# Row normalisation of attention probabilities moved from GpSimd to VectorE, in a two-layer decoder trunk on one Trainium2 core

## The chip, the core and the metric

The kernel runs on one core of one Trainium2 chip. A core has TensorE (PE, matrix products; its weight loads are listed as PEld), VectorE (DVE), ScalarE (ACT), GpSimd (POOL) and SyncE (SP, which only issues transfers here). They run side by side, each with its own queue of instructions in a fixed order, and wait for one another through semaphores. The metric is the time of the whole kernel on the device in microseconds (us).

## The reference

Two residual layers on x of 1024 positions x 1024 channels, fp32: a gated short convolution, and then forgetting attention with 16 heads of 64. The change is in the second. Per head and block of 128 queries:

```python
s = jnp.einsum('bhqd,bhkd->bhqk', qb, k) * scale
s = s + cb[..., :, None] - c[..., None, :]
s = jnp.where(kpos[None, :] <= qpos[:, None], s, neg)
p = jax.nn.softmax(s, axis=-1)
return jnp.einsum('bhqk,bhkd->bhqd', p, v)
```

`c` is a running sum of log forget gates. Before it lie an RMS norm and one projection to q, k, v, an output gate z and the forget gates, q and k being RMS-normalised per head; behind it the gating by silu(z) and an output projection that is added to x.

## The kernel before, in words

Every fp32 product is made from three TensorE products: an operand is split into a "hi" part (rounded, made by ScalarE) and a "lo" part (the rest, a subtraction on VectorE or GpSimd). So each tile of weights, h, probabilities, q, k and v has a hi and a lo.

The attention layer is software-pipelined over head pairs. Iteration `it` (0 to 8) projects q, k, z and v of pair `it` (`proj`, iterations 0 to 7) and does the attention of pair `it` - 1 (`att`, iterations 1 to 8); iterations 2 to 6 or 7 are a hardware loop on each engine. A pass has 8 steps `i`: four for each of the two heads of the pair ("side"), with query super-blocks t = 3, 2, 1, 0 of 256 rows, each as two blocks `par` 0 and 1 of 128 queries, whose rows have 128 (2t + 1 + par) keys: 896 and 1024 columns in steps 0 and 4, 640 and 768 in 1 and 5, 384 and 512 in 2 and 6, 128 and 256 in 3 and 7.

What happens to a block (step i, block par): TensorE makes the scores in PSUM (L722). VectorE adds the mask (L1657) and takes the negated row maximum (L1663). ScalarE takes the exponential into `p_big` (even steps) or `p_small` (odd steps) and sums each row into `denom` (L1170). VectorE inverts it (`invert`, L1671, semaphore `s_rd`), and GpSimd multiplies the row by the inverse (`normalise`, L1934, semaphore `s_pn`). In the next step TensorE transposes the normalised blocks in chunks of 256 keys (L739, waits for `s_pn` of both blocks), ScalarE makes `pt_hi` (L1180), VectorE makes `pt_lo` (`pt_low`, L1677), and TensorE multiplies by v, "pv" (L758, waits for `s_ptl`). ScalarE and VectorE collect the output (L1190, L1684), and VectorE gates it (L1693).

In each step TensorE's queue has, in this order: scores of block 0, two or three pieces of projection (L575), transposes of the previous step's first two chunks, more projection, in steps 2 to 5 the head mean squares (L774, L775), scores of block 1, and then pv, transposes and projection in turn. VectorE's queue has mask and maximum of block 0, an evacuation of a projection (L1735, L1749), `invert` of block 0, the first `pt_low`, mask and maximum of block 1, the other `pt_low`, the gating, `invert` of block 1, and in steps 2 to 5 a Newton refinement (`refine`, L1714 to L1722) of the head norms, in whose middle the mask and maximum of the next step's block 0 are put:

```python
if att:
    invert(it, i, 0)
for c in range(min(2, chunks)):
    pt_low(own, at, c)
```

GpSimd's queue has per pass the 16 `normalise`, four `w_low` (lo part of a weight tile, L1925), four `square_lo` (L1939) and two `stack_k_lo` (L1945). At the end of iteration 7 VectorE makes h_lo of four gated output tiles (`y2_low`, L1807), and GpSimd two in iteration 8 (L1952). All loads are issued by SyncE.

Of the kernel before, what the change touches and what calls it, by code (L numbers as in the profile page):

```python
# [7 lines left out]
ALU = mybir.AluOpType  # L8
# [3 lines left out]
P = 128  # L12
# [13 lines left out]
N_FORGET, N_AIN, N_AOUT = 0, 1, 4 * KT + 1  # L26
# [33 lines left out]
STEPS = [(x, t) for x in range(2) for t in (3, 2, 1, 0)]  # L60
# [4 lines left out]
def keys(t, par):  # L65

    return P * (2 * t + 1 + par)
# [48 lines left out]
def hybrid(nc, x, w_cin, w_cout, w_ain, w_forget, w_aout, conv_gain, conv_taps, attn_gain, b_forget,  # L116
# [5 lines left out]
    with ExitStack() as ctx:  # L122
# [23 lines left out]
        rdenom = sb("rdenom", [P, 4])  # L146
# [44 lines left out]
        p_big = sb("p_big", [P, 2, S])  # L191
# [31 lines left out]
        p_small = sb("p_small", [P, 2, 3 * P * 2])  # L223
# [54 lines left out]
        s_wlo = sem("w_lo_made")  # L278
# [30 lines left out]
        s_rd = sem("denominators_inverted")  # L309
        s_pn = sem("p_normalised")  # L310
# [1028 lines left out]
        def _(dve):  # L1339
# [325 lines left out]
            def invert(it, i, par):  # L1665
                pair = it - 1
                col = 2 * (i % 2) + par
                dve.wait_ge(s_exp, 16 * pair + 2 * i + par + 1)
                if counted(16 * pair + 2 * i + par - 3):
                    dve.wait_ge(s_pn, 16 * pair + 2 * i + par - 3)  # L1670
                v.reciprocal(rdenom[:, col:col + 1], denom[:, col:col + 1]).then_inc(s_rd, 1)  # L1671

            def pt_low(it, at, c):
                pair = it - 1
                g, w = CHUNK0[at] + c, chunk_columns(STEPS[at][1], c)
                dve.wait_ge(s_pth, CHUNKS * pair + g + 1)
                TT(pt_lo[:, g % 2, 0:w], ps[:, B_PT + g % 2, 0:w], pt_hi[:, g % 2, 0:w].bitcast(F32),  # L1677
                   ALU.subtract).then_inc(s_ptl, 1)
# [72 lines left out]
            def iteration(it, proj, att, before, base, last=False):  # L1751
                local = 0
                for i in range(8):
                    own, at = (it, i - 1) if i else (it - 1, 7)
                    chunks = STEPS[at][1] + 1 if (att and i) or (before and not i) else 0
                    if att and not (proj and 3 <= i <= 6):
                        row_max(it, i, 0)
                    if att and i == 0:
                        vz_evac(it - 1, 7)
                    if proj and 1 <= i <= 4:  # L1760
                        qk_evac(it, i - 1)
                    if proj and 5 <= i:
                        vz_evac(it, i - 1)
                    if not proj and i == 2:
                        add_ahead(1)
                    if not proj and i > 2:
                        add_ahead(i - 1)
                    if att:
                        invert(it, i, 0)
                    for c in range(min(2, chunks)):  # L1770
                        pt_low(own, at, c)
                    if att and i == 0:
                        v_low(it - 1, 0)
                    if att:
                        row_max(it, i, 1)
                    if not proj and i == 1:
                        y2_low(6)
                    if att and i == 0:
                        stack_q_lo(it - 1, 1)
                    if att and i == 1:  # L1780
                        v_low(it - 1, 1)
                    for c in range(2, chunks):
                        pt_low(own, at, c)
                    if att and i and STEPS[i - 1][1] in (1, 3) and (i >= 2 or (before and proj)):
                        out_gate(*((it, i - 2) if i >= 2 else (it - 1, 7)))
                    if att:
                        invert(it, i, 1)
                    if proj and 2 <= i <= 5:
                        local = refine(it, i - 2, base, local, i + 1 if att else None)
                    if not att and i in (1, 3, 4, 5):  # L1790
                        forget((1, 3, 4, 5).index(i))
                    if proj and i == (6 if last else 7):
                        stack_q_lo(it, 0)
                    if last and i == 7:
                        for k in range(4):
                            y2_low(k)
                    if chunks and STEPS[at][1] % 2 == 0:
                        out_sum(own, at)
                    if not proj and i == 0:
                        out_gate(it - 1, 7)  # L1800
                    if not proj and i == 1:
                        add_ahead(0)
                return local
# [50 lines left out]
        def _(pool):  # L1854
            g = nc.gpsimd
            TT = g.tensor_tensor
# [68 lines left out]
                TT(w_lo[slot][:, :, :], w_raw[:, slot, :, :], w_hi[slot][:, :, :].bitcast(F32),  # L1925
                   ALU.subtract).then_inc(s_wlo, 1)

            def normalise(it, i, par):
                pair = it - 1
                w = keys(STEPS[i][1], par)  # L1930
                col = 2 * (i % 2) + par
                pool.wait_ge(s_rd, 16 * pair + 2 * i + par + 1)
                p = (p_big if i % 2 == 0 else p_small)[:, par, 0:w]
                TT(p, p, rdenom[:, col:col + 1].broadcast_to([P, w]), ALU.mult).then_inc(s_pn, 1)  # L1934

            def square_lo(it, u):

                pool.wait_ge(s_qsq, 4 * it + u + 1)
# [15 lines left out]
            def iteration(it, proj, att):  # L1954
                for i in range(8):
                    if proj and i % 2 == 0:
                        w_low(N_AIN + 4 * it + i // 2 + 1, (N_AIN + i // 2 + 1) % 2)
                    if not proj and i in (3, 5, 7):
                        n = N_AOUT + 2 + (3, 5, 7).index(i)
                        w_low(n, n % 2)  # L1960
                    if not proj and i == 0:
                        y2_low(4)
                    if att:
                        normalise(it, i, 0)
                    if not proj and i == 0:
                        y2_low(5)
                    if att and i == 1 and proj:
                        pool.wait_ge(s_pn, 16 * it - 13)
                        stack_k_lo(it - 1, 1)
                    if not proj and i == 2:  # L1970
                        pool.wait_ge(s_pn, 16 * it - 11)
                        stack_k_lo(it - 1, 1)
                    if proj and i == 7:
                        if att:
                            pool.wait_ge(s_pn, 16 * it - 1)
                        else:
                            pool.wait_ge(s_wlo, N_AIN + 4 * it + 5)
                        stack_k_lo(it, 0)
                    if att:
                        normalise(it, i, 1)  # L1980
                    if proj and 1 <= i <= 4:
                        square_lo(it, i - 1)
                    if not proj and i == 0:
                        w_low(N_AOUT + 1, (N_AOUT + 1) % 2)
# [50 lines left out]
```

## Time and profile before

| | |
|---|---|
| median of 3 runs | 1135.32 us (1134.02 to 1135.85) |
| profiled execution | 1135.81 us, of which the span is 1134.0 us |
| granted TensorE clock, mean | 0.992 |
| busy: PE, PEld, DVE, ACT, POOL | 1106.5, 916.7, 770.9, 601.4, 565.3 us |

The span is the time from the first to the last instruction. "Busy" counts the time in which an engine works on an instruction. Idle time of an engine costs only where another engine, in the end TensorE, waits for what it makes. The convolution layer fills the first 434 us; iteration 1 begins near 482 us, and the seven passes with both a projection and attention (iterations 1 to 7) last until about 1004.

### The profile page before, as it was taken

To read this page: it belongs to the slowest core of one execution; us is meant where nothing else is said; L and a number is where in the kernel's file an instruction comes from. 1 tells how busy PE (TensorE), PEld (TensorE's weight loads), DVE (VectorE), ACT (ScalarE), POOL (GpSimd) and SP (SyncE) were. 2 spreads that over 40 slices of the span, in tenths; PEclk is the share of its full clock that TensorE was granted. 3 is DMA by queue.
4 is the path that set the end of the run, shared out by engine and by line. 5 is a ranking of instruction groups with operands and counts; after the bars stand their busy time and mean duration, and the time that the engine had idled before them with its cause. 6 is when DMAs were issued, how large, how long until landed. Compare 5 with 4: busy or idle time off the path is not lost.

```text
span 1134.0 us, 16593 instructions
## 1 busy us (share of the span) xinstructions
PE 1106.5 (98%) x5512; PEld 916.7 (81%) x5512; DVE 770.9 (68%) x1180; ACT 601.4 (53%) x1014; POOL 565.3 (50%) x376
## 2 busy tenths in 40 slices
PE   4999999999999999999999999999999999989998
PEld 3787888888888887788888888888888888878887
DVE  5896787567766325667777777686776777876641
ACT  5553233233243324675766767767667676666510
POOL 2235665555563646454555554645546555554420
PEclk8999999999999999999999999999999999989999
DMA  6202101210135402110100110101001101002142
GB/s 223 75 1 75 43 33 75 75 62 14 75 107 174 130 39 93 45 41 20 38 21 19 38 38 19 37 19 38 19 18 38 38 19 37 19 23 90 56 167 75
DMA packets 20257, 64.17 MB, mean 57 GB/s; under 512 B 2928, under 2 KB 3056, under 8 KB 20208
## 3 DMA queue, kind: packets, MB, share of 16 engines
q1 hardware_dynamic: 20064, 63.53, 16.6%
q8 instruction: 28, 0.46, 0.2%
q14 instruction: 21, 0.17, 0.0%
q10 hardware_dynamic: 144, 0.00, 0.0%
HBM read 54.88 MB, written 8.65 MB: 56 GB/s over the span
## 4 chain that ended last, share of the span: by engine, by line
PE 80%; DVE 7%; issue 2%; POOL 2%; ACT 1%; DMA 1%; SPq 0%; ACTq 0%; DVEq 0%; POOLq 0%
PE ps L575 34%; PE ps L589 18%; PE ps L670 6%; PE ps L722 6%; PE ps L758 6%; PE ps L739 6%; POOL p_big L1934 1%; DVE neg_max L1663 1%; PE ps L781 1%; DVE b_lo L1381 1%; DVE h_lo L1807 1%; PE ps L774 1%; PE ps L775 1%; PE ps L694 1%; DMA raw<-in_w_cout 1%
## 5 line engine op out<-in xcount | busy, mean ns | idle before, releaser
L575 PE MATMUL ps<-h_hi,w_hi 128*128 128x512 f32 x632 | 262.9, 416 | 4.0 <-DVE v_t L1749 2.1
L575 PE MATMUL ps<-h_hi,w_lo 128*128 128x512 f32 x632 | 248.6, 393 | 0.0
L575 PE MATMUL ps<-h_lo,w_hi 128*128 128x512 f32 x632 | 248.3, 393 | 0.0
L1870 POOL TENSOR_TENSOR a_lo<-raw,a_hi 128x512 fp32r<-128x512 f32 x94 | 136.7, 1466 | 155.4 <-ACT a_hi L954 155.4
L589 PE MATMUL ps<-b_hi,a_hi 128*128 128x512 f32 x456 | 179.8, 394 | 9.1 <-DVE b_lo L1381 8.5
L589 PE MATMUL ps<-b_lo,a_hi 128*128 128x512 f32 x456 | 178.5, 391 | 0.0
L589 PE MATMUL ps<-b_hi,a_lo 128*128 128x512 f32 x456 | 178.4, 391 | 0.0
L1934 POOL TENSOR_TENSOR p_big<-p_big,rdenom 128x896 f32<-128x896 f32 (+1 forms) x64 | 94.1, 1470 | 96.3 <-DVE rdenom L1671 96.2
L575 PEld LDWEIGHTS ps<-h_hi,w_lo 128*128 128x128 f32 x632 | 118.9, 188 | 27.2
L1934 POOL TENSOR_TENSOR p_small<-p_small,rdenom 128x640 f32<-128x640 f32 (+1 forms) x64 | 72.1, 1127 | 135.4 <-DVE rdenom L1671 135.1
L575 PEld LDWEIGHTS ps<-h_hi,w_hi 128*128 128x128 f32 x632 | 119.6, 189 | 20.9 <-DVE v_t L1749 3.0
L575 PEld LDWEIGHTS ps<-h_lo,w_hi 128*128 128x128 f32 x632 | 119.8, 190 | 14.7 <-issue 0.2
L1925 POOL TENSOR_TENSOR w_lo<-w_raw,w_hi 128x1024 fp32r<-128x1024 f32 x39 | 95.0, 2435 | 62.8 <-ACT w_hi L926 62.8
L954 ACT ACTIVATE a_hi<-raw 128x512 fp32r<-128x512 f32 x94 | 58.1, 628 | 118.5 <-DMA raw<-in_w_cin 44.5
L1677 DVE TENSOR_TENSOR pt_lo<-ps,pt_hi 128x512 fp32r<-128x512 f32 (+1 forms) x160 | 96.7, 629 | 34.6 <-ACT pt_hi L1180 34.0
L589 PEld LDWEIGHTS ps<-b_hi,a_hi 128*128 128x128 f32 x456 | 86.2, 189 | 31.0 <-DVE b_lo L1381 10.9
L589 PEld LDWEIGHTS ps<-b_hi,a_lo 128*128 128x128 f32 x456 | 86.2, 189 | 18.1
L589 PEld LDWEIGHTS ps<-b_lo,a_hi 128*128 128x128 f32 x456 | 86.2, 189 | 17.8 <-issue 0.2
L1663 DVE TENSOR_REDUCE neg_max<-ps 128x1 f32<-128x896 f32 (+7 forms) x128 | 97.0, 758 | 4.4
L1180 ACT ACTIVATE pt_hi<-ps 128x512 fp32r<-128x512 f32 (+1 forms) x160 | 83.1, 551 | 23.8 <-PE ps L739 21.9
L722 PE MATMUL ps<-k,q 128*128 128x512 f32 (+5 forms) x384 | 92.1, 348 | 0.6 <-ACT p_big L1170 0.6
L1657 DVE TENSOR_TENSOR ps<-ps,mask_bf 128x128 f32<-128x128 f32 x128 | 38.0, 297 | 67.1 <-PE ps L722 66.7
(179 smaller groups left out, 2063.7 us busy)
## 6 DMA issues: line engine op xcount, KB each, us to landing
w_raw<-in_w_ain SPq DMA_DIRECT2D x32, 512.0 KB, 3.3
raw<-in_w_cin SPq DMA_DIRECT2D x28, 512.0 KB, 4.3
xy<-in_x SPq DMA_DIRECT2D x16, 512.0 KB, 4.5
raw<-in_w_cout SPq DMA_DIRECT2D x8, 512.0 KB, 4.2
x_dram<-xy SPq DMA_DIRECT2D x8, 512.0 KB, 4.0
w_raw<-in_w_aout SPq DMA_DIRECT2D x8, 512.0 KB, 3.3
out<-y SPq DMA_DIRECT2D x7, 512.0 KB, 7.1
raw<-in_w_cin SPq DMA_DIRECT2D x8, 256.0 KB, 8.6
```

The costliest lines, as they stand in the source:

```text
L575: last = mm(ps[:, bank, :], st[slot][:, k, :], mov(k)[:, halves(h)], start=(at == 0 and (when or k == 0) and st is w_hi and mov is mov_hi) ...
L589: ins = mm(ps[:, bank, :], st[:, i % RING, k, :], mov[:, k, :], start=(first and st is a_hi and mov is b_hi[b]), stop=(last and st is a_lo ...
L670: ins = mm(ps[:, BANKS[u % 8], :], st[:, i, k % KH, :], mov[Y_SLOT + s][:, 2 * c + h, :], start=(first and k == ks[0] and st is a_hi and m ...
L722: last = mm(ps[:, bank, 0:w], a[:, side, qs:qs + P], b[:, side, c * w:(c + 1) * w], start=(a is q1), stop=(a is q2))
L739: last = nc.tensor.transpose(ps[:, B_PT + g % 2, at:at + P], src[:, par, (2 * c + kp) * P:(2 * c + kp + 1) * P], ident[:, :])
L758: last = mm(ps[:, B_OUT, at + skip:at + 2 * P], v_st[:, side, 2 * c + kp, :], mov[:, g % 2, kp * 2 * P:(kp + 1) * 2 * P - skip], start=(c ...
L1180: A(pt_hi[:, g % 2, 0:w], ps[:, B_PT + g % 2, 0:w], ACT.Copy).then_inc(s_pth, 1)
L1663: v.tensor_reduce(neg_max[:, col:col + 1], src, ax, ALU.max, negate=True).then_inc(s_max, 1)
L1677: TT(pt_lo[:, g % 2, 0:w], ps[:, B_PT + g % 2, 0:w], pt_hi[:, g % 2, 0:w].bitcast(F32), ALU.subtract).then_inc(s_ptl, 1)
L1870: TT(a_lo[:, i % RING, :, :], entry_source(i), a_hi[:, i % RING, :, :].bitcast(F32), ALU.subtract).then_inc(s_alo, 1)
L1925: TT(w_lo[slot][:, :, :], w_raw[:, slot, :, :], w_hi[slot][:, :, :].bitcast(F32), ALU.subtract).then_inc(s_wlo, 1)
L1934: TT(p, p, rdenom[:, col:col + 1].broadcast_to([P, w]), ALU.mult).then_inc(s_pn, 1)
```

## The change

`normalise` leaves GpSimd's queue and becomes a `tensor_scalar` of VectorE, issued directly behind each `invert`. It waits for VectorE's own reciprocal (`s_rd`) and counts `s_pn` as before. On GpSimd, three waits for `s_pn` ahead of `stack_k_lo` become waits for earlier `w_low` of the same queue.

```diff
 (VectorE)
+            def normalise(it, i, par):
+                pair = it - 1
+                w = keys(STEPS[i][1], par)
+                col = 2 * (i % 2) + par
+                dve.wait_ge(s_rd, 16 * pair + 2 * i + par + 1)
+                p = (p_big if i % 2 == 0 else p_small)[:, par, 0:w]
+                TS(p, p, rdenom[:, col:col + 1], None, ALU.mult).then_inc(s_pn, 1)
...
                     if att:
                         invert(it, i, 0)
+                        normalise(it, i, 0)
...
                     if att:
                         invert(it, i, 1)
+                        normalise(it, i, 1)
 (GpSimd)
-            def normalise(it, i, par):
-                pair = it - 1
-                w = keys(STEPS[i][1], par)
-                col = 2 * (i % 2) + par
-                pool.wait_ge(s_rd, 16 * pair + 2 * i + par + 1)
-                p = (p_big if i % 2 == 0 else p_small)[:, par, 0:w]
-                TT(p, p, rdenom[:, col:col + 1].broadcast_to([P, w]), ALU.mult).then_inc(s_pn, 1)
...
-                    if att:
-                        normalise(it, i, 0)
...
                     if att and i == 1 and proj:
-                        pool.wait_ge(s_pn, 16 * it - 13)
+                        pool.wait_ge(s_wlo, N_AIN + 4 * it + 2)
                         stack_k_lo(it - 1, 1)
                     if not proj and i == 2:
-                        pool.wait_ge(s_pn, 16 * it - 11)
+                        pool.wait_ge(s_wlo, N_AOUT + 2)
                         stack_k_lo(it - 1, 1)
                     if proj and i == 7:
-                        if att:
-                            pool.wait_ge(s_pn, 16 * it - 1)
-                        else:
-                            pool.wait_ge(s_wlo, N_AIN + 4 * it + 5)
+                        pool.wait_ge(s_wlo, N_AIN + 4 * it + 5)
                         stack_k_lo(it, 0)
-                    if att:
-                        normalise(it, i, 1)
```

## Rows read from the trace of the kernel before

**Rows 1.** The page's part 1: busy us, share of the span, instructions.
```profile
PE 1106.5 (98%) x5512; PEld 916.7 (81%) x5512; DVE 770.9 (68%) x1180; ACT 601.4 (53%) x1014; POOL 565.3 (50%) x376
```

**Rows 2.** Table of stretches, 677 to 752 us: length, busy by engine, clock, DMA.
```profile
677.00:752.00 75.00, 74.74 (x419) 63.30 (x418) 54.98 (x104) 52.15 (x91) 40.24 (x26) 1.00 0.09 28
```

**Rows 3.** Waits, 527 to 1010 us (total, times, longest); a piece of the chain.
```profile
PEld ps L739 <- POOL p_big L1934: 4.8, 7, 0.7
...
677.66 2.29 POOL p_big L1934
```

**Rows 4.** Groups by shape on VectorE: busy us, mean ns of one | idle before.
```profile
L1663 DVE TENSOR_REDUCE neg_max<-ps 128x1 f32<-128x1024 f32 x16 | 19.6, 1224 | 0.5
...
L1663 DVE TENSOR_REDUCE neg_max<-ps 128x1 f32<-128x384 f32 x16 | 8.9, 557 | 0.6
```

**Rows 5.** Line L1489 (least, median, most ns); timeline near 116 us: start, duration.
```profile
L1489 DVE TENSOR_SCALAR ca<-ubuf,taps x8: 753/754/1669, 78.5 to 342.9; 128x1024 f32<-128x1024 f32 x8
...
115.16 3.97 POOL L1870 TENSOR_TENSOR a_lo<-s_t,a_hi 128x512 fp32r<-128x512 f32 x2
...
116.31 1.67 DVE L1489 TENSOR_SCALAR ca<-ubuf,taps 128x1024 f32<-128x1024 f32 x1
```

**Rows 6.** Timeline of step 0, 708 to 715 us.
```profile
708.28 2.38 POOL L1925 TENSOR_TENSOR w_lo<-w_raw,w_hi 128x1024 fp32r<-128x1024 f32 x1 [2.49 <-ACT w_hi L926]
...
709.70 0.16 DVE L1671 RECIPROCAL rdenom<-denom 128x1 f32<-128x1 f32 x1 [0.82 <-ACT p_big L1170]
709.99 0.56 DVE L1677 TENSOR_TENSOR pt_lo<-ps,pt_hi 128x384 fp32r<-128x384 f32 x1
...
711.52 0.27 PE L758 MATMUL ps<-pt_hi,v_st 128*128 128x256 f32 x1
...
711.96 0.29 DVE L1657 TENSOR_TENSOR ps<-ps,mask_bf 128x128 f32<-128x128 f32 x1
...
714.88 0.59 PEld L722 LDWEIGHTS ps<-k,q 128*128 128x128 f32 x4 [0.42 <-ACT p_big L1170]
```

**Rows 7.** Timeline of steps 4 and 5, 748 to 759 us.
```profile
748.18 0.54 DVE L1677 TENSOR_TENSOR pt_lo<-ps,pt_hi 128x384 fp32r<-128x384 f32 x1
...
749.12 0.28 PE L758 MATMUL ps<-pt_hi,v_st 128*128 128x256 f32 x1
...
752.15 0.16 DVE L1671 RECIPROCAL rdenom<-denom 128x1 f32<-128x1 f32 x1 [1.27 <-ACT p_big L1170]
...
752.39 2.28 POOL L1934 TENSOR_TENSOR p_big<-p_big,rdenom 128x1024 f32<-128x1024 f32 x1 [2.38 <-DVE rdenom L1671]
...
754.64 1.27 POOL L1939 TENSOR_TENSOR sq_lo<-sq_raw,sq_hi 128x512 fp32r<-128x512 f32 x1
...
754.73 1.09 PE L739 MATMUL ps<-ident,p_big 128*128 128x128 f32 x8 [0.26 <-POOL p_big L1934]
...
757.29 1.26 DVE L1677 TENSOR_TENSOR pt_lo<-ps,pt_hi 128x512 fp32r<-128x512 f32 x2
...
758.24 0.28 PE L758 MATMUL ps<-pt_hi,v_st 128*128 128x256 f32 x1
```

**Rows 8.** Timeline of step 6, 764 to 769 us.
```profile
764.24 0.30 DVE L1657 TENSOR_TENSOR ps<-ps,mask_bf 128x128 f32<-128x128 f32 x1 [0.32 <-PE ps L722]
...
767.10 1.27 DVE L1677 TENSOR_TENSOR pt_lo<-ps,pt_hi 128x512 fp32r<-128x512 f32 x2
...
768.13 0.28 PE L758 MATMUL ps<-pt_hi,v_st 128*128 128x256 f32 x1
```

**Rows 9.** Timeline at the way into iteration 8, 1002 to 1015 us.
```profile
1002.68 7.21 DVE L1807 TENSOR_TENSOR h_lo<-y,h_hi 128x1024 fp32r<-128x1024 f32 x4
1002.84 1.51 POOL L1934 TENSOR_TENSOR p_small<-p_small,rdenom 128x256 f32<-128x256 f32 x1 [0.83 <-DVE rdenom L1671]
1005.12 2.56 POOL L1952 TENSOR_TENSOR h_lo<-y,h_hi 128x1024 fp32r<-128x1024 f32 x1 [0.76 <-ACT h_hi L1321]
...
1011.88 0.50 PE L575 MATMUL ps<-h_hi,w_hi 128*128 128x512 f32 x1 [2.09 <-DVE v_t L1749]
```

## The prediction, made before the changed kernel was run

> **What bounds the kernel now.** I read the page's busy times first [rows 1]: TensorE (PE) is busy 98% of the 1134.0 us of the span, so a change off TensorE can only give back the little that TensorE waits, or make it wait more. Then the table of stretches [rows 2]: in the 75 us from 677 to 752, one pass of the attention loop, TensorE is busy 74.74 us, VectorE (DVE) 54.98 and GpSimd (POOL) 40.24, with the clock at 1.00. VectorE looks free for 20 us of a pass; whether it is free at the places where TensorE is due is another question. Third, the chain that ended last and the table of waits [rows 3]: the chain goes through GpSimd's normalise at 677.66, a pass later the same instruction starts at 752.39 [rows 7], 74.73 us on, and in the seven full passes TensorE's weight loads wait for it 4.8 us in all, 7 times, 0.7 us at the longest. That is the only place at which the moved work is on the path today.
>
> **What is taken away.** GpSimd loses 16 multiplications a pass; the 1024-wide one of step 4 takes 2.28 us [rows 7]. Only one of them has TensorE waiting behind it. It is this one: it ends at 754.67, and the eight transposes start at 754.73 with 0.26 us of idle before them. The projection matmul before them would have freed TensorE some 0.42 us earlier, counted by the spacing of the starts (0.65 us where 0.23 is usual). So the gain is at most 0.42 x 7, and 0.4 in the last pass: 3.3 us.
>
> **What is added.** VectorE gets a TENSOR_SCALAR of the same width behind each reciprocal. The same form exists in the trace: a [128 x 1024] fp32 tensor in SBUF times a [128 x 1] column, L1489, 754 ns at the median and 753 at the least [rows 5]. A reduce of 1024 columns takes 1224 ns and one of 384 columns 557 ns [rows 4], which is 1.04 ns a column, so L1489 at 754 ns must be passing about two columns in that time: 0.52 x 1024 = 533 ns plus 221 fixed. By this the widths cost 896: 0.69, 1024: 0.75, 640: 0.55, 768: 0.62, 384: 0.42, 512: 0.49, 128: 0.29, 256: 0.35 us, together 8.3 us a pass for both heads. That takes VectorE to 63 of 75 us. Bounds: if all of the 754 ns went with the columns (0.74 ns each), 6.8 us; if narrow or in-place forms fell back to one column per 1.04 ns (the reduce), about 12 us. I take 8.3, because L1489 is the same instruction with the same operand kinds. An inserted one moves what is behind it by its duration and 0.02 us.
>
> The Trainium skill ("VectorE: DVE Perf Modes", The perf-mode tier table) has fp32 tensor_scalar in SBUF at two elements a cycle and tensor_tensor at one; an estimate by its figures (about 158 cycles fixed, 0.96 GHz) is 0.69 us for 1024 columns, where the trace has 0.754. With 0.06 less for each, the sum below would be some 2 us smaller.
>
> **A lock.** One of the eight L1489 took 1669 ns [rows 5]. It started at 116.31, GpSimd's two subtractions ran from 115.16 for 3.97 us, so the first ended near 117.15, and 117.15 + 0.75 + 0.08 is 117.98, where L1489 ended. The row shows an instruction of the added kind standing still until GpSimd's running one ends. I price that below.
>
> The Trainium skill ("SBUF — State Buffer", Who interferes with whom) says of this pair that whoever starts first holds a shared port for its whole instruction. This trace agrees (1.67 for 0.75 us). If the two shared the port evenly instead, the first term below would be nearly nothing, and the sum 3 us smaller.
>
> **Walking one pass.** I call the steps 0 to 7; each has two blocks of scores (a and b). TensorE's order is fixed, so a late input stops it.
>
> Step 0 [rows 6]. The reciprocal of 0a ends at 709.86. GpSimd's w_lo holds the lock from 708.28 to 710.66, so the 896-wide multiply ends at 711.4 and not 710.6. The pt_lo behind it (0.56 us, old start 709.99) ends at 711.95; TensorE wants it at 711.52. v_lo (0.69) follows, and the mask of 0b starts at 712.44, not 711.96. The mask, the reduce, the exponential and then the scores of step 1 (714.88, which already wait for that exponential) form one chain, so step 1 starts 0.48 us late. With the lock free the multiply would end before 710.6 and nothing would be late. The 1024-wide one of 0b falls where VectorE has idle time in steps 0 and 1, and the steps 1, 2 and 3 have slack against the pv matmuls of 0.3 us and more: nothing, or up to 0.05.
>
> Steps 4 and 5 [rows 7]. The 896-wide multiply delays pt_lo from 748.72 (748.18 + 0.54) to 749.43, and TensorE, due at 749.12, stops 0.3 us; that is used up by the 0.42 us which the normalise of GpSimd no longer costs before the transposes. Then comes the place that decides. From the reciprocal of 4b at 752.15 to the pt_lo at 757.29, in front of which no idle time is marked, VectorE works through without a wait: Newton steps, mask, reduce, output sum, evacuation of a projection, reciprocal of 5a. The first pt_lo of step 4's result ends at 757.29 + half of 1.26 = 757.92, and TensorE uses it at 758.24: slack 0.32 us. Into this run go the multiply of 4b (0.75 + 0.02) and of 5a (0.55 + 0.02), and about 0.04 is inherited: 1.38. TensorE is 1.38 - 0.32 = 1.06, with the handing over 1.1 us late. The 0.42 us is inside this figure, since it is taken against the old start.
>
> Step 6 [rows 8]. VectorE's lateness of 1.38 grows by the 768-wide multiply (0.64) to 2.02; the mask of 6a had 0.32 us of idle before it, which goes: 1.7. With the 384-wide multiply (0.44) the next pt_lo is 2.15 late: its first half ended at 767.10 + 0.63 = 767.73, now 769.9. TensorE, due at 768.13 and already 1.1 late, would come at 769.23: another 0.7 us. Step 7 has wide waits for ScalarE's osum and for GpSimd's k_lo, which now comes earlier: nothing.
>
> So 0.48 + 1.1 + 0.7 = 2.3 us a pass, in seven passes 16 us.
>
> The way into the eighth pass [rows 9]. Four h_lo run on VectorE in 7.21 us, 1.8 each, and TensorE waits for what is behind them (2.09 us for v_t). GpSimd's normalise at 1002.84 (1.51 us) got between them and goes; GpSimd's second h_lo, which stood behind the first normalise of iteration 8, now can follow the one of 1005.12 directly. If it gets the lock between VectorE's, that is up to 2.1 us more, otherwise nothing: I take 1. In the eighth pass there is no Newton work and VectorE waits often; 0.4 gained, about 0.3 lost at a pt_lo. Nothing.
>
> What only moves: GpSimd's w_lo, sq_lo and k_lo no longer stand behind a normalise. They start earlier, TensorE waits for none of them today, and no DMA is late for them. The two waits that stood for "normalised" now ask for GpSimd's previous w_lo, on its own queue: nothing.
>
> **The rivals.**
> (a) All is hidden. VectorE's 20 idle us [rows 2] speak for it, the idle-free run of rows 7 against it. Then the 3.3 us are won: 1132.5 us. It decides if the multiplies of 4b and 5a together take under 0.3 us more than what they replace, against 1.34 here.
> (b) Only step 0 loses, 0.48 x 7 = 3.4 against 3.3 gained: 1135.5, no change. It needs slack in rows 7 that I do not see.
> (c) The multiplies run at one column per 1.04 ns. Then 1024 and 640 cost 1.22 and 0.82, 768 and 384 0.96 and 0.56: 0.74 more in step 5, 0.5 more in step 6, 0.4 more in step 0, 1.6 a pass and 11 in all: 1164. Against it: L1489.
> (d) The lock bites once more. GpSimd's sq_lo (1.27 us, rows 7) can start as soon as ScalarE is done, about 1.15 us after the reciprocal of 4b, and the Newton product behind the multiply starts about 0.9 after it. A quarter of a us decides; if sq_lo is first, the run of rows 7 loses up to 1.27 more a pass, 9 in all: 1161.
> That the multiply isn't moved cannot be: GpSimd's queue has none left.
>
> **The numbers.** The profiled execution took 1135.8 us, of which 1134.0 are the span; the median of the runs is 1135.3, 0.5 less. 1135.8 + 16 + 1 = 1152.8, less 0.5 is 1152.3. I say 1152.5, with a chance of 0.7 for this case, its own range 1145 (narrow multiplies at 0.74 ns a column, 0.3 less a pass, step 0's term at half, nothing at the eighth pass) to 1157. (c) and (d) get 0.1 each, (a) and (b) 0.05 each. The range 1143 to 1163 leaves out (a), (b) and the end of (c). A measurement of this kernel tells about 0.2% (2.3 us) from no change. Slower 0.9, same 0.05, faster 0.05.
>
> **What would show it.** After: L1489's neighbour in the list of groups, a TENSOR_SCALAR of 128 on VectorE, at 0.75 us for 1024 and 0.42 for 384; GpSimd's busy time in a stretch of 75 us far under 40, VectorE's at 63 or a little less (its pass is longer); passes of about 77 us instead of 74.7; waits of TensorE's pv matmuls (L758's place) for pt_lo, largest behind steps 4 and 5, and none for a normalise. Wrong would be: passes of 74.3 us (then VectorE hid it), or multiplies of 1.2 us.

## The result, and the profile of the changed kernel

The changed kernel takes 1152.62 us at the median of four runs (1150.99 to 1153.24), the kernel before 1134.83 us at the median of four (1134.02 to 1135.85). The ratio is 1.0157, with a 95% interval from 1.0145 to 1.017: it is slower by 17.8 us. The forecast was 1152.5 us. Two executions of the kernel before that were taken beside experiments 4 to 6 (1224.29 and 6273.82 us) were in a slower state and are left out everywhere.

The page's first lines of the kernel after, to be read beside [rows 1]:

```profile
span 1149.2 us, 16484 instructions
...
PE 1111.3 (97%) x5512; PEld 913.5 (79%) x5512; DVE 845.3 (74%) x1308; ACT 600.6 (52%) x1014; POOL 405.8 (35%) x248
```

VectorE (DVE) has 128 instructions and 74 us more, GpSimd (POOL) 128 fewer and 160 us less. TensorE (PE) does the same 5512. A reader who looks for the engine with the most work finds nothing that explains 18 us: the work became less in sum, and VectorE is still a quarter idle.

A row of the table of stretches of the kernel after, one pass long (length, busy by engine, clock, DMA), beside [rows 2]:

```profile
677.00:754.00 77.00, 75.41 (x417) 62.68 (x416) 64.23 (x121) 51.76 (x90) 19.73 (x10) 1.00 0.09 28
```

The next two stretches of 77.00 us hold the same instructions, so a pass now lasts 77.0 us and not 74.75. The clock is at 1.00 as before. TensorE is busy 75.41 of 77.00 us, where it was busy 74.74 of 75.00: it now waits 1.6 us a pass (some of the matmuls behind a wait are shown longer). The list of groups gives what was added, as busy us, mean ns of one | idle before:

```profile
L1679 DVE TENSOR_SCALAR p_small<-p_small,rdenom 128x768 f32<-128x768 f32 x16 | 14.8, 924 | 0.6
L1679 DVE TENSOR_SCALAR p_big<-p_big,rdenom 128x384 f32<-128x384 f32 x16 | 12.4, 775 | 0.6
L1679 DVE TENSOR_SCALAR p_big<-p_big,rdenom 128x1024 f32<-128x1024 f32 x16 | 12.1, 754 | 0.6
```

The 1024-wide one costs 754 ns, as L1489 did [rows 5]. The means of 768 and 384 columns are higher than what those widths need, because some of these multiplies stood still behind a GpSimd instruction (the lock of the prediction); in the timeline the free ones take 0.62 and 0.42 us. Last the waits from 470 to 1030 us (total, times, longest), which replace [rows 3]:

```profile
PEld ps L758 <- DVE pt_lo L1685: 21.0, 37, 1.3
...
PE ps L758 <- DVE pt_lo L1685: 10.3, 21, 1.1
```

No wait for a normalised row is left. TensorE now waits for pt_lo, the low part of the previous step's probabilities: 21 waits of its matmuls, three in each of seven passes, and 37 of its weight loads. Where they lie, the timeline of the kernel after shows (start, duration, idle before and its releaser):

```profile
744.13 1.15 DVE L1685 TENSOR_TENSOR pt_lo<-ps,pt_hi 128x512 fp32r<-128x512 f32 x2
...
744.87 0.19 PEld L758 LDWEIGHTS ps<-pt_hi,v_st 128*128 128x128 f32 x1 [0.22 <-DVE pt_lo L1685]
...
754.41 0.39 PE L758 MATMUL ps<-pt_hi,v_st 128*128 128x256 f32 x1 [0.20 <-DVE pt_lo L1685]
...
764.32 0.39 PE L758 MATMUL ps<-pt_hi,v_st 128*128 128x256 f32 x1 [1.02 <-DVE pt_lo L1685]
...
774.72 0.39 PE L758 MATMUL ps<-pt_hi,v_st 128*128 128x256 f32 x1 [0.25 <-DVE pt_lo L1685]
```

These are steps 3, 4, 5 and 6, and the wait of step 5 is the long one. The work of VectorE ahead of it, from the timeline of the same kernel:

```profile
757.09 0.16 DVE L1671 RECIPROCAL rdenom<-denom 128x1 f32<-128x1 f32 x1 [1.27 <-ACT p_big L1170]
757.29 0.76 DVE L1679 TENSOR_SCALAR p_big<-p_big,rdenom 128x1024 f32<-128x1024 f32 x1
757.96 0.68 DVE L1722 TENSOR_TENSOR newton<-y 128x512 f32<-128x512 f32 x1
...
763.12 0.55 DVE L1679 TENSOR_SCALAR p_small<-p_small,rdenom 128x640 f32<-128x640 f32 x1
763.59 1.28 DVE L1685 TENSOR_TENSOR pt_lo<-ps,pt_hi 128x512 fp32r<-128x512 f32 x2
```

From the reciprocal to pt_lo it was 5.14 us before (752.15 to 757.29 [rows 7]) and is 6.50 now: 1.36 more, with not a moment idle in between, and 1.27 us idle ahead of it that nothing could use, since the reciprocal waits for the exponential.

**Step by step.** In what follows the length of a step is the distance in TensorE's timeline from its scores of block a (L722) to those of the next step, in the pass that begins at 705.75 us before and at 710.35 us after. I use this table for every kernel:

| us | step 0 | 1 | 2 | 3 | 4 | 5 | 6 | 7 | pass |
|---|---|---|---|---|---|---|---|---|---|
| before | 9.13 | 11.24 | 9.46 | 8.18 | 8.58 | 11.33 | 8.98 | 7.85 | 74.75 |
| after | 9.15 | 11.32 | 9.43 | 8.42 | 9.03 | 12.16 | 9.49 | 8.00 | 77.00 |
| growth | 0.02 | 0.08 | -0.03 | 0.24 | 0.45 | 0.83 | 0.51 | 0.15 | 2.25 |

Seven passes of 2.25 us are 15.8 us. From the first scores of iteration 8 to the last piece of the chain it was 93.86 us before (1004.36 to 1098.22) and is 95.40 after (1017.98 to 1113.38): 1.5 more. Together 17.3 us, where the medians differ by 17.8.

### The profile page after: what moved, and what is told of

The parts are those of the page before. It is cut to its first block, busy times and chain, and to the rows that moved or that the text cites. A ratio compares the mean times of both kernels' runs of the same rounds, so it can differ in the third digit from the quotient of the medians.

```text
span 1149.2 us, 16484 instructions
## 1 busy us (share of the span) xinstructions
PE 1111.3 (97%) x5512; PEld 913.5 (79%) x5512; DVE 845.3 (74%) x1308; ACT 600.6 (52%) x1014; POOL 405.8 (35%) x248
## 4 chain that ended last, share of the span: by engine, by line
PE 78%; DVE 13%; issue 6%; ACT 2%; DMA 1%; POOL 0%; DVEq 0%; ACTq 0%; SPq 0%; POOLq 0%
PE ps L575 27%; PE ps L589 26%; PE ps L670 8%; PE ps L758 6%; PE ps L722 4%; PE ps L739 4%; DVE neg_max L1663 2%; DVE pt_lo L1685 2%; DVE ps L1728 1%; DVE ps L1657 1%; PE ps L781 1%; DVE newton L1722 1%; DVE y L1757 1%; DVE h_lo L1817 1%; PE ps L694 1%
## 5 line engine op out<-in xcount | busy, mean ns | idle before, releaser
L589 PEld LDWEIGHTS ps<-b_lo,a_hi 128*128 128x128 f32 x456 | 86.2, 189 | 17.8 <-issue 0.2
L758 PE MATMUL ps<-pt_hi,v_st 128*128 128x256 f32 x320 | 83.3, 282 | 13.3 <-DVE pt_lo L1685 13.1
L1941 POOL TENSOR_TENSOR sq_lo<-sq_raw,sq_hi 128x512 fp32r<-128x512 f32 x32 | 43.6, 1361 | 142.2 <-ACT sq_hi L1298 142.2
L722 PE MATMUL ps<-k,q 128*128 128x512 f32 (+5 forms) x384 | 92.0, 348 | 1.1 <-ACT p_big L1170 0.3
L1947 POOL TENSOR_TENSOR k<-kn,k 64x1024 fp32r<-64x1024 f32 x16 | 38.3, 2394 | 145.8 <-ACT k L1210 145.8
```

The costliest lines, as they stand in the source:

```text
L589: ins = mm(ps[:, bank, :], st[:, i % RING, k, :], mov[:, k, :], start=(first and st is a_hi and mov is b_hi[b]), stop=(last and st is a_lo ...
L722: last = mm(ps[:, bank, 0:w], a[:, side, qs:qs + P], b[:, side, c * w:(c + 1) * w], start=(a is q1), stop=(a is q2))
L758: last = mm(ps[:, B_OUT, at + skip:at + 2 * P], v_st[:, side, 2 * c + kp, :], mov[:, g % 2, kp * 2 * P:(kp + 1) * 2 * P - skip], start=(c ...
```

## The experiments

The theory that I call place: what counts is the time of VectorE's idle-free runs between the reciprocal of a block b and the next pt_lo, step by step; a multiply elsewhere is free. Its rivals: load (VectorE's total work, wherever it stands) and lock (what costs is that VectorE's new instructions and GpSimd's hold each other up). All kernels were measured with the kernel before beside them.

**1. Part of the blocks back on GpSimd (mid_gpsimd, mid_vector).** Each block's multiply was given to one engine by a list, numbered 2i + par, with a semaphore for either engine. In mid_gpsimd only 4b, 5a, 5b and 6a (of 16) are GpSimd's; mid_vector is the reverse.

```diff
+BY_V = [0, 1, 2, 3, 4, 5, 6, 7, 8, 13, 14, 15]     # mid_gpsimd
+BY_V = [9, 10, 11, 12]                             # mid_vector
...
             def normalise(it, i, par):
+                if 2 * i + par not in BY_V:
+                    return
```

> Twelve multiplications a pass stay on VectorE; those of 4b, 5a, 5b and 6a go back to GpSimd. Place theory (the loss is made where VectorE runs without idle time from the reciprocal of 4b to the pt_lo of steps 5 and 6): most of the loss goes, 0.3 to 0.6 us a pass stay, 1137 to 1139 us. Load theory (VectorE's total work makes the loss, in proportion): 5.9 of the 8.3 us of multiplications a pass stay on it, so 0.7 of 17.8, 1147 us. Lock theory (the multiplications wait for GpSimd's instructions): GpSimd has more to run, no gain, 1150 or more.

> The counterpart: only 4b, 5a, 5b and 6a are on VectorE, twelve on GpSimd. Place theory: 1.0 us late at the first pt_lo of step 5, 0.7 more at step 6, 1.7 us a pass, 1146 to 1147 us. Load theory: 0.3 of 17.8, 1140 us. Lock theory: it depends on what GpSimd runs beside them, which in steps 4 to 6 is little: 1136 to 1140.

Measured: mid_gpsimd 1140.57 us against 1134.89, ratio 1.0053 (1.0039 to 1.0066); mid_vector 1148.12, ratio 1.012 (1.0105 to 1.0136). Twelve multiplies on VectorE cost 5.7 us, the other four alone 13.2. That is the wrong way round for load; the lock theory is out as well, with 1150 or more expected of mid_gpsimd and at most 1140 of mid_vector. mid_gpsimd is some 2 us above what I expected, and its step table says why: steps 3 and 4 stay at 8.42 and 9.06 as in the kernel after, while step 5 is 11.08. The waits of mid_vector (470 to 1030 us; the lines of this kernel are shifted, L774 is pv and L790 a head mean square) showed a second customer of the same run:

```profile
PE ps L774 <- DVE pt_lo L1704: 9.0, 14, 1.1
...
PE ps L790 <- DVE kn L1749: 1.9, 7, 0.3
```

VectorE's refined k (kn) stands in that run too, and TensorE's next head mean square waits for it: both use one PSUM buffer, and the kernel has a semaphore there. One more thing is in mid_vector's steps. Its step 4 does not grow (8.60 us) and its step 5 is 12.66, together 21.26; the kernel after has 9.03 and 12.16, together 21.19. What TensorE loses in step 4 of the kernel after it would have waited in step 5 anyway, so the two steps have one cost and not two.

**2. Block a's multiply behind the first two pt_lo (pt_first).** Nothing is taken from VectorE, two neighbours change places.

```diff
                     if att:
                         invert(it, i, 0)
-                        normalise(it, i, 0)
                     for c in range(min(2, chunks)):
                         pt_low(own, at, c)
+                    if att:
+                        normalise(it, i, 0)
```

> All sixteen on VectorE; block a's multiplication comes behind the first two pt_lo of its step and not ahead of them. Place theory: the pt_lo of step 4's result in step 5 is late by 4b's multiply alone, 0.8 less 0.3 of slack; at step 6 VectorE is late by 2.0 less the 0.3 of idle, and TensorE stops for 1.3 us a pass in all instead of 2.3: 1144 to 1146 us. Load and lock theories: the work and what it collides with stay, 1151 to 1153.

Measured: 1143.8 us (1142.67 to 1144.73), ratio 1.008 (1.0066 to 1.0094). Half of the loss is gone by order alone, with VectorE's work unchanged; load and lock, which both gave 1151 to 1153, fall here too. Steps 3 and 4 are back at 8.15 and 8.57 us, the kernel before's own lengths: their growth came from the multiplies of 3a and 4a in front of pt_lo. Step 5 stays long (11.99) and so does step 6 (9.43).

**3. GpSimd's w_lo made to start later (w_lo_later).** In step 0 and 2 GpSimd's w_lo waits until VectorE has multiplied block a, so that the lock is free.

```diff
+                    if proj and i in (0, 2) and att:
+                        pool.wait_ge(s_pn, 16 * (it - 1) + 2 * i + 1)
```

> As the changed kernel, but GpSimd starts the w_lo of steps 0 and 2 only when that step's block a is normalised, so that neither stands in front of a multiplication. Place theory: these blocked multiplications lie where there is slack; no difference, 1151.5 to 1153. Lock theory: the multiplications of 0a, 1b and 2a are 0.4, 0.8 and 0.7 us over their free durations; some of it comes back, 3 to 13 us less, 1139 to 1149.

Measured: 1152.09 us (1149.79 to 1152.88), ratio 1.015 (1.0136 to 1.0164), a pass of 76.96 us. The multiply of 0a took 0.69 us in this kernel's timeline, where it takes 1.09 us in the kernel after, and the time did not move. So the lock on 0a and 2a is worth nothing. The run leaves others: 1b still stands behind GpSimd's sq_lo (1.44 us), and nothing is changed in iteration 8, where the lock does cost (see below).

**4. One multiply more, at two places (extra_5a, extra_6b).** A second multiplication of the same row, by a column of ones, directly ahead of the normalising one of 5a (640 columns) or of 6b (512 columns).

```diff
+                if 2 * i + par == 10:               # 13 in extra_6b
+                    TS(p, p, ones_col[:, :], None, ALU.mult).then_inc(s_one, 1)
+                    dve.wait_ge(s_one, pair + 1)
```

> As the changed kernel, with one more multiplication (by 1.0) of the 640-wide block of 5a on VectorE, ahead of its normalise, 0.55 us a pass. Place theory: it lies in the run without idle time and TensorE waits behind it, so all of it shows, 0.57 x 7 = 4.0 us, 1156.6. Load theory: as for the same size anywhere (next run).

> The same, with the 512-wide block of 6b, 0.49 us a pass. Behind it VectorE is idle for 1.95 us. Place theory: no difference to the changed kernel, 1152 to 1153. Load theory: as much as 5a's, 0.49 x 7 = 3.4 us, 1156.

Measured beside the kernel before at 1134.22 us: extra_5a 1156.85 us (1156.35 to 1157.16), extra_6b 1152.09 (1151.0 to 1152.58). At 5a the pass grows by 0.65 us over the kernel after (77.65), most of it in step 5 (12.74, +0.58, where the multiply takes 0.55); at 6b it is 77.00, unchanged. Nearly the same instruction costs its whole duration at one place and nothing at another. This is the clearest of the runs. The whole kernel took 4.8 us more with extra_5a than with extra_6b: 7 x 0.65, and what it adds in iteration 8.

**5. A single block moved (one_vector).** Only 4b is VectorE's, `BY_V = [9]`.

> Only 4b's multiplication is on VectorE, the one for which TensorE waits in the kernel before; fifteen stay on GpSimd. Place theory: the 0.42 us of waiting go, but the pt_lo of step 5 is late by 0.77 less 0.32: 0.45 us a pass more than before, 3 us, 1138. Rival: the waiting that goes counts alone, 1131.5.

Measured: 1140.18 us (1139.04 to 1141.47), ratio 1.0052 (1.004 to 1.0065). I had expected 1138: step 5 grew by 0.75 us, not by 0.45. The mean square's wait for kn is in this kernel as well (1.9 us in 7 waits), as in mid_vector; I had counted the slack of pt_lo only. So one multiply of 0.75 us in this run costs 0.75 us a pass, although the transposes no longer wait for GpSimd.

**6. A cheaper multiply on GpSimd? (gpsimd_ts).** The kernel before, with GpSimd's form changed from a product of two tensors (one of them a column, broadcast) to tensor_scalar. GpSimd's hardware loop over iterations is written out in it.

```diff
-                TT(p, p, rdenom[:, col:col + 1].broadcast_to([P, w]), ALU.mult).then_inc(s_pn, 1)
+                g.tensor_scalar(p, p, rdenom[:, col:col + 1], None, ALU.mult).then_inc(s_pg, 1)
```

> All sixteen on GpSimd as before, but as a tensor_scalar with the inverse as scalar operand and not as a tensor_tensor with the inverse broadcast (GpSimd's loop over iterations 2 to 7 is written out). If this form reads one stream and is quicker, the 1024-wide one ends 0.4 us or more earlier and the wait at the transposes of step 4 goes: 1131 to 1132.5 us. If it takes as long: 1134.8.

Measured: 1148.09 us (1147.68 to 1148.42), ratio 1.0122 (1.0106 to 1.0137). Neither expectation: it is slower. First the group of this kernel, then the same group in the kernel before:

```profile
L1965 POOL TENSOR_SCALAR p_big<-p_big,rdenom 128x1024 f32<-128x1024 f32 x16 | 48.2, 3011 | 30.4 <-DVE rdenom L1688 30.4
```

```profile
L1934 POOL TENSOR_TENSOR p_big<-p_big,rdenom 128x1024 f32<-128x1024 f32 x16 | 33.0, 2064 | 42.4 <-DVE rdenom L1671 42.4
```

3.01 us instead of 2.06 for the same multiplication. TensorE waits 11.3 us for it from 470 to 1030 us, in 14 waits, two a pass: step 5 grows by 0.97 us to 12.30, and step 1, which did not wait for GpSimd before, by 0.50 to 11.74. So of these two the form that the kernel before uses on GpSimd is the quicker one.

**7. Two Newton instructions of step 4 ahead of the reciprocal (ahead_after, ahead_pt_first).** The idle 1.27 us before the reciprocal of 4b is filled with the first two instructions of the Newton work that stood behind it (1.4 us); ahead_pt_first has the reordering of run 2 as well.

```diff
+                    if att and proj and i == 4:
+                        for part in range(2):
+                            refine_head(it, i - 2, base, local, part)
                     if att:
                         invert(it, i, 1)
                         normalise(it, i, 1)
```

> The changed kernel, but the first two instructions of the Newton work of step 4 (the product y0*y0 and the one behind it, 1.4 us together) stand ahead of the reciprocal of block 4b, where VectorE otherwise has 1.27 us without work; nothing is taken away from any engine. Place theory: the load between that reciprocal and step 5's pt_lo falls by some 1.3 us, so TensorE no longer waits 1.0 us there; step 4 keeps its growth of 0.45 us and step 3 its 0.24; a pass of about 75.5 us (before 74.75, after 77.0), in all 1138 to 1143 us. Load theory (VectorE carries 8.3 us more a pass, wherever): as the changed kernel, 1152 us.

> As ahead_after, and the multiply of block a stands behind the first two pt_lo of its step instead of ahead of them. Place theory: the growth of steps 3 and 4 goes as well (pt_first alone showed them at 8.15 and 8.57 us), the multiply on GpSimd that held the transposes is absent, so a pass of 74.3 to 74.8 us and 1131 to 1135 us in all, which would be at or under the kernel before though VectorE does all 16 multiplications of a pass. Load theory: 1144 us, as pt_first.

Measured beside the kernel before at 1134.93 us (1132.72 to 1136.66): ahead_after 1147.22 us (1146.07 to 1148.58), ratio 1.011 (1.0095 to 1.0124); ahead_pt_first 1135.52 us (1133.33 to 1137.87), ratio 1.0005 (0.9996 to 1.0014). Their steps:

| us | step 0 | 1 | 2 | 3 | 4 | 5 | 6 | 7 | pass |
|---|---|---|---|---|---|---|---|---|---|
| ahead_after | 9.16 | 11.33 | 9.45 | 8.42 | 9.02 | 11.37 | 9.49 | 7.98 | 76.22 |
| ahead_pt_first | 9.16 | 11.32 | 9.45 | 8.15 | 8.59 | 10.82 | 9.39 | 8.01 | 74.89 |

The direction is place's, and load (1152 and 1144) falls; but ahead_after kept 0.7 us a pass more than I had expected. The timeline of VectorE in it shows why:

```profile
757.31 0.16 DVE L1671 RECIPROCAL rdenom<-denom 128x1 f32<-128x1 f32 x1
757.51 0.75 DVE L1679 TENSOR_SCALAR p_big<-p_big,rdenom 128x1024 f32<-128x1024 f32 x1
758.69 0.30 DVE L1657 TENSOR_TENSOR ps<-ps,mask_bf 128x128 f32<-128x128 f32 x1 [0.43 <-PE ps L722]
...
763.01 1.28 DVE L1685 TENSOR_TENSOR pt_lo<-ps,pt_hi 128x512 fp32r<-128x512 f32 x2
```

1.4 us went ahead, but the mask of 5a then had to wait 0.43 us for TensorE's scores, and the reciprocal itself came 0.04 us later in the pass. The run to pt_lo shrank from 6.50 to 5.70 us, and step 5 by 0.79. With all 16 multiplies on VectorE, ahead_pt_first ends up within 0.2% of the kernel before: reordering VectorE's queue gives back 17.2 of the 17.8 us. That is not quite the same as saying that the move costs nothing in a good order, because the same reordering of the Newton work also makes the kernel before faster, as run 8 shows; against ahead_before (1132.17 us) the 16 multiplies still cost 3.4 us, 0.54 us a pass. Of the waits for pt_lo it has 0.3 us in 2 (470 to 1030 us), where the kernel after has 10.3 in 21. It does not get below the kernel before, which I had thought possible: steps 1, 6 and 7 keep 0.65 us (0.08 + 0.41 + 0.16), against 0.51 gained in step 5.

**8. The same in the kernel before (ahead_before, product_before).** GpSimd normalises; in step 4 the two Newton instructions, or only the first of them (the product y0*y0), stand ahead of the reciprocal.

> The kernel before (GpSimd normalises), with the first two Newton instructions of step 4 ahead of the reciprocal of 4b. In the kernel before the Newton product starts beside GpSimd's 1024-wide multiply, which takes 2.28 us there and 1.89 us where nothing of the kind runs beside it. Place theory with a gap at GpSimd: the multiply ends some 0.4 us sooner, the transposes of step 4 no longer wait; 0.4 x 7 or 8, so 1131.5 to 1132.5 us. If the order of VectorE's work is worth nothing there, 1134.8 us.

> As ahead_before, with only the first of the two, the product y0*y0, ahead of the reciprocal; it is the only one of the two whose two inputs both lie in SBUF. If it alone held GpSimd's multiply: the same as ahead_before, 1131.5 to 1132.5 us. If the second one (input in PSUM) matters as well: between that and 1134.8 us.

Measured: ahead_before 1132.17 us (1130.83 to 1134.32, 11 runs), ratio 0.9978 (0.9969 to 0.9987); product_before 1131.51 (1129.93 to 1134.05, 10 runs), ratio 0.9976 (0.9966 to 0.9985). Both are faster than the two kernels of the case, by 2.8 and 3.4 us, and the same within their intervals. In both only step 5 changes, from 11.33 to 10.94 us, and the pass from 74.75 to 74.35 and 74.33. GpSimd's multiply of 4b is the reason, here in product_before:

```profile
749.45 1.90 POOL L1947 TENSOR_TENSOR p_big<-p_big,rdenom 128x1024 f32<-128x1024 f32 x1 [2.37 <-DVE rdenom L1671]
```

```profile
749.31 0.70 DVE L1719 SCALAR_TENSOR_TENSOR ps<-ps,newton 128x512 f32<-128x512 f32 x1
```

It takes 1.90 us where it took 2.28 [rows 7]. VectorE's second Newton instruction, with an input in PSUM, still starts just ahead of it and runs beside it; so it was the product, both of whose inputs lie in SBUF, that had held it in the kernel before.

**All of them beside their passes.** The growth of the pass, seven times; what the stretch from the first scores of iteration 8 to the last piece of the chain grew by (93.86 us in the kernel before); their sum; and the difference of the medians:

| kernel | pass, us | 7 x growth | last stretch | sum | measured |
|---|---|---|---|---|---|
| after | 77.00 | 15.8 | 1.5 | 17.3 | 17.8 |
| mid_gpsimd | 75.53 | 5.5 | 1.4 | 6.9 | 5.7 |
| mid_vector | 76.66 | 13.4 | 1.2 | 14.6 | 13.2 |
| pt_first | 76.06 | 9.2 | 0.0 | 9.2 | 8.9 |
| w_lo_later | 76.96 | 15.5 | 1.9 | 17.4 | 17.2 |
| extra_5a | 77.65 | 20.3 | 2.1 | 22.4 | 22.6 |
| extra_6b | 77.00 | 15.8 | 1.7 | 17.5 | 17.9 |
| one_vector | 75.53 | 5.5 | 0.1 | 5.6 | 6.0 |
| gpsimd_ts | 76.53 | 12.5 | 1.3 | 13.8 | 13.9 |
| ahead_after | 76.22 | 10.3 | 1.6 | 11.9 | 12.3 |
| ahead_pt_first | 74.89 | 1.0 | -0.1 | 0.9 | 0.6 |
| ahead_before | 74.35 | -2.8 | 0.3 | -2.5 | -2.8 |
| product_before | 74.33 | -2.9 | -0.5 | -3.4 | -3.4 |

Sum and measurement agree to 0.5 us, except for the two kernels of run 1, which came out 1.2 and 1.4 us better. Two things in the traces can account for it. Seven times one pass is a little too much for mid_gpsimd: from the first scores of iteration 1 to those of iteration 8 it takes 527.27 us, the kernel before 522.45, which is 4.8 and not 5.5. And iteration 1, ahead of which all these kernels do the same work, begins anywhere from 479.07 us (w_lo_later) to 482.93 us (ahead_pt_first), so a single trace can't settle differences of 1 us.

**The last stretch: place and lock together.** Taken step by step, the last stretch grows at two places, behind 5a and behind 7a of the second head. In the kernel after, its distance from the first scores of iteration 8 is 0.12 us less than before at the scores of 5b, 0.52 more at those of 6a, still 0.52 more at those of 7b, and 1.54 at the end. The other kernels tell the two apart. Wherever VectorE has 7a ahead of pt_lo (after, mid_gpsimd, w_lo_later, extra_5a, extra_6b, ahead_after) the part behind the scores of 7b grows by 1.02 to 1.05 us; wherever GpSimd has it, or it stands behind pt_lo, by 0.02 at most. Free, the multiply of 7a would take 0.29 us and VectorE stood idle for longer than that there; in the kernel after it takes 1.84, because GpSimd's w_lo runs from 1089.72 to 1092.12. These are the pt_lo that it delays, in the kernel before and after, and TensorE's wait for it:

```profile
1076.71 1.15 DVE L1677 TENSOR_TENSOR pt_lo<-ps,pt_hi 128x512 fp32r<-128x512 f32 x2 [0.53 <-ACT pt_hi L1180]
```

```profile
1092.12 1.14 DVE L1685 TENSOR_TENSOR pt_lo<-ps,pt_hi 128x512 fp32r<-128x512 f32 x2
...
1092.95 0.36 PE L758 MATMUL ps<-pt_hi,v_st 128*128 128x256 f32 x1 [0.81 <-DVE pt_lo L1685]
```

So here the lock costs about 1 us, once, and some part of the half us at 5a (1.14 us there instead of 0.55, behind the w_lo of 1071.42). Putting the multiply behind pt_lo takes both away: the last stretch is 93.85 us in pt_first and 93.81 in ahead_pt_first. This is read from the timelines; no run took the lock alone away in iteration 8.

## Why the prediction was right, step by step

The total was right to 0.1 us, and the mechanism (late pt_lo behind an idle-free run of VectorE) is what the profile and the experiments show for the seven passes. That the total came out to 0.1 us is luck: the terms were off by up to 1.8 us, some high and some low.

- **What a multiply costs.** 0.754 us for 1024 columns was predicted as 0.75, and free ones of 896, 768, 640, 512, 384, 256 and 128 columns show 0.69, 0.62, 0.55, 0.49, 0.42, 0.35 and 0.29 in the timeline: all as predicted from L1489 and the slope of half a reduce. The sentence on the Trainium skill ("VectorE: DVE Perf Modes", The perf-mode tier table) would have put each 0.06 us lower (its 1227 ns for 2048 elements give 154 fixed cycles, not 158, and 0.69 us); the measurement decides for 0.75, while two elements a cycle, its rule, agrees with the slope. Rival (c), one column per 1.04 ns, is out.
- **Step 0: predicted 0.48 us, measured 0.02.** This is the largest error within a pass. The multiply was to end 0.74 us after GpSimd's w_lo let go (711.4 against 710.66). The timeline of the kernel after:

```profile
712.73 2.38 POOL L1935 TENSOR_TENSOR w_lo<-w_raw,w_hi 128x1024 fp32r<-128x1024 f32 x1 [8.25 <-ACT w_hi L926]
```

```profile
714.51 1.09 DVE L1679 TENSOR_SCALAR p_big<-p_big,rdenom 128x896 f32<-128x896 f32 x1
715.52 0.55 DVE L1685 TENSOR_TENSOR pt_lo<-ps,pt_hi 128x384 fp32r<-128x384 f32 x1
715.99 0.68 DVE L1711 TENSOR_TENSOR v_st<-ps,v_st 128x512 fp32r<-128x512 f32 x1
716.59 0.28 DVE L1657 TENSOR_TENSOR ps<-ps,mask_bf 128x128 f32<-128x128 f32 x1
```

  w_lo ends at 715.11 and the multiply at 715.60, 0.49 us later, not 0.74; w_lo also ended 0.15 us earlier against the pass. So v_st started at 715.99, 5.64 us into the pass, against 5.60 before (711.35 - 705.75), where it had waited 0.81 us for ScalarE. The mask moved by 0.03 us. With the lock free (run 3) step 0 is as long. That the multiply is blocked was right; that this costs anything there was not. The price came from a reading of [rows 5]: the prediction let the first of GpSimd's two subtractions end near 117.15, half of 3.97 us after 115.16. Taken alone it lasts longer (kernel before):

```profile
115.16 2.27 POOL L1870 TENSOR_TENSOR a_lo<-s_t,a_hi 128x512 fp32r<-128x512 f32 x1
```

  It ended at 117.43, so L1489 ended 0.55 us after it and not 0.83: a held multiply needs less than its free 0.75 us once it is released, and that row already showed it.
- **Steps 1 to 3: predicted nothing, or 0.05; measured 0.29.** Step 3 has 0.24 of it. The narrowest multiply (3a, 0.29 us) stands in front of the pt_lo at 744.13, which is 33.78 us into the pass and was at 33.40; the slack I had read there, 0.3 us, was used up. pt_first takes it away.
- **Steps 4 and 5: predicted 1.1, measured 1.28** (0.45 + 0.83). The added time in the idle-free run, 1.38, was 1.36. The pv matmul of step 5 was to be 0.48 + 1.1 = 1.58 us later within its pass and is 1.48 later (764.32 - 710.35 against 758.24 - 705.75 [rows 7]). Of this the runs add something the prediction lacked: kn is wanted as early as pt_lo (one_vector, mid_vector).
- **Step 6: predicted 0.7, measured 0.51, and step 7 0.15 instead of nothing.** The pass: predicted 2.3, measured 2.25. Five errors of 0.15 to 0.5 us cancelled, which is luck.
- **The gain of 0.42 us** at the transposes of step 5 came: 1.97 us from the scores of 5a to them, 2.39 before. What it really was, only run 8 showed: not the length of GpSimd's multiply as such but VectorE's product in front of it. It can be had without the change.
- **The way into the eighth pass: predicted 1, measured -0.3.** From the first scores of iteration 8 to the matmul that v_t releases it was 7.52 us (1004.36 to 1011.88) and is 7.24 (1017.98 to 1025.22). VectorE's four h_lo take 6.80 us instead of 7.21. The prediction had given GpSimd's second h_lo up to 2.1 us there; none of it came.
- **The eighth pass: predicted nothing, measured 1.5 together with the way into it, so about 1.8 by itself.** This is the largest error of all. Two multiplies of a block a (5a and 7a) are in the chain of the kernel after (start, duration):

```profile
1073.02 1.14 DVE p_small L1679
...
1090.36 1.84 DVE p_small L1679
```

  Both hold up the pt_lo behind them, and both are longer than a free one of their width (0.55 and 0.29), each beside a w_lo of GpSimd. The prediction took VectorE's waiting there as cover. The idle time was there (0.53 us ahead of the pt_lo of 7a in the kernel before), but the lock, which the prediction had not looked for in this pass, used it up. In pt_first, with the multiply of block a behind pt_lo, the 1.5 us are gone.

The rivals: (a), all hidden (its 1132.5 should read 1132.0, 1135.3 less 3.3), and (b), only step 0, would be passes at or about 74.75 us; both are out, and (b)'s own step is the one that costs nothing. (d), GpSimd's sq_lo ahead of the Newton product, did not happen: the product started at 757.96 and sq_lo at 758.32, in this row of the kernel after, to be read beside the rows of step 4 above:

```profile
758.32 1.48 POOL L1941 TENSOR_TENSOR sq_lo<-sq_raw,sq_hi 128x512 fp32r<-128x512 f32 x1 [5.92 <-ACT sq_hi L1298]
```

It was held 0.2 us itself (1.27 free [rows 7]).

What stays open: why steps 1, 6 and 7 keep 0.65 us in ahead_pt_first was not tested, and how the half us at 5a in iteration 8 divides between the multiply and the lock was not either.

## What to carry to other kernels

Price a moved instruction by the run it lands in: find the engine's last idle time before the next result that the busiest engine is due to use, add up what stands between, and compare it with the slack; here 8.3 us of extra work a pass cost 2.25 us in one order and 0.14 in another, or 0.54 against a kernel before that has the better order too. Put what the bounding engine waits for first and what nobody needs until the next step behind it, and put work that waits for nothing into the idle time ahead of a waiting instruction. Before moving work off a slow engine, look whether a neighbour holds it up at that place: moving one 0.69 us product gained 3.4 us, where moving all 16 multiplies lost 17.8. And when you read a duration off a merged row, ask for its parts one by one.

## What the runs showed of the hardware

- A VectorE multiply that is held by GpSimd's running instruction ends sooner after its release than its free duration: 0.49 us after for 896 columns (0.69 free), 0.08 us after for 128 columns (0.29 free; w_lo 1089.72 + 2.40 = 1092.12, the multiply 1090.36 + 1.84 = 1092.20). The two differ by 0.53 ns a column. The other held ones fit: 0.55 us after for 1024 columns (L1489), 0.42 for 768 (1b: sq_lo 730.18 + 1.29, the multiply 730.46 + 1.43), 0.35 for 640, 0.22 for 384 (2a). Each is about 0.20 us less than its free duration, as if that much of an instruction's fixed part passed during the wait. The other way round, VectorE's product of two SBUF tensors held GpSimd's multiply (2.28 us, 1.90 without it). The Trainium skill ("SBUF — State Buffer", Who interferes with whom) names both cases and says that the first to start keeps the shared pair for its whole instruction; these numbers agree.
- On GpSimd, tensor_scalar with a [128 x 1] column is slower than tensor_tensor with that column broadcast: means of 16 of 3.01 against 2.06 us at 1024 columns, 2.53 against 1.68 at 896, 1.89 against 1.26 at 640 (gpsimd_ts and the kernel before).
- An instruction with an input in PSUM (the second Newton instruction, 0.70 us) ran beside GpSimd's multiply without holding it: 1.90 us, where the same width took 1.89 us alone in step 0 of the kernel before (715.19).
